# Two attention layers without staged operands: masks added ahead by GpSimd, values in the transposes' bank, pool mixing in halves, branches merged by tile pairs

## The chip, the cores and the metric

The kernel runs on 1 core of one Trainium2 chip. The metric is device time in microseconds for one execution. Engines: TensorE (PE, with its weight loads as PEld), VectorE (DVE), ScalarE (ACT), GpSimd (POOL) and SyncE (SP), which issues the stream of weights. Each engine executes its own queue in order, and engines wait for each other by semaphores.

## What is computed

The reference runs two layers of a first block (256 tokens, width 1024) and then one layer of a second block. The change lies in the first block, of which this is the core:

```python
for l in range(DEPTH):                       # 2 layers
    h = rms_norm(x, norm_g[l])
    proj = h @ w_in[l]
    (pool_u, pool_z, aq, ak, av, az, iq, ik, iw, mq, mz, gates) = jnp.split(proj, split_points, axis=-1)
    y_pool = multi_scale_pool(pool_u, pool_w[l], pool_scale[l]) * silu(pool_z)
    # 8 heads of 64; the indexer picks 64 of the admissible keys of each token
    y_attn = dsa_attention(aq, ak, av, iq, ik, iw, rel_bias) * silu(az)
    mk, mv = split(rms_norm(mem, mem_norm_g[l]) @ w_mem_kv[l])
    y_mem = memory_attention(mq, mk, mv) * silu(mz)          # 4 heads of 128
    g = sigmoid(gates)                                        # 3 x 1024 columns
    merged = g0 * (y_pool @ w_branch[l, 0]) + g1 * (y_attn @ w_branch[l, 1]) + g2 * (y_mem @ w_branch[l, 2])
    x = x + merged @ w_out[l]
```

The attention's logits are q k / 8 plus a bias by relative position, with keys that the indexer did not pick masked out. multi_scale_pool takes trailing means over 2, 4, 8 and 16 tokens and maps each group of 128 channels by its own matrix.

## The kernel before

**The weight stream.** All weights of 1024 rows come as blocks of 128 columns (512 KB) through four slots. A block goes through a fixed chain: SyncE loads raw[s]; ScalarE converts it to the rounded upper part w_hi (split_hi, L264); VectorE forms the rest w_lo (split_lo, L270); TensorE makes 24 matmuls of 256 tokens with it (block_cols): h_hi and h_lo by w_hi (L284, L285) and h_hi by w_lo (L299). Conversions run two blocks ahead (`ahead`): in step s of a group of four, ScalarE and VectorE convert the block of slot s + 2. ScalarE or VectorE takes the result out of PSUM (evac, L345). For tokens in rows, block_rows takes two slots at once (L330 to L335), and evac_rows takes its two results out one after the other, each behind the conversion of its own step.

**A layer** has 20 groups G to G + 19 of four blocks: index queries, q (qT), k (kT), v; the gates az, pz, mz; the pool's input pu; memory queries (mqT); then six groups for the 24 gate blocks, beside which the softmax of the six pairs runs: four pairs of attention heads (hp) and two pairs of memory heads (mp); then three groups of branch blocks, which need y_hi and y_lo; then two groups of w_out.

**A pair** runs so. GpSimd copies q and k of the pair into `stage` (st_q, st_k, L437 and L438), behind its own pooling (L418 to L432) for the first pair of a layer. TensorE forms the logits in PSUM banks 0 and 1 (free_ps[0], free_ps[1]; L1417, L1419) and adds the mask by a matmul with an identity (L1418, L1420), then three gate blocks, the transposes of the probabilities into banks 2 and 3 (L1428), the fourth gate block, and the values into bank 0 (L1434 to L1436). VectorE converts the lower part of slot 2, adds the bias to the logits (L999, L1001, four instructions), takes the row maxima; ScalarE makes the exponentials (L618), evicts the first gate block, converts slot 3; VectorE makes the lower part of slot 3 and normalises (L982). ScalarE copies the transposed probabilities to SBUF. After the values, VectorE multiplies them with the gate az (L1012) and splits the product into y_hi and y_lo; the next pair's logits wait for that product (pv_used). Between the fourth and fifth pair, TensorE mixes the pool (L1442) and VectorE takes that out (L1022).

**The branches.** For each of twelve blocks VectorE multiplies the result with the gate into `soft` (L1053) and GpSimd adds that to `merged` (L453), which it cleared before. All branch blocks wait for all six y's and for all gates. At the end ScalarE rounds `merged` in two halves into hS_hi (L654), VectorE forms hS_lo (L1060), and first_blocks starts w_out with two blocks, half by half (L318 is its lower part). Then VectorE adds each w_out result to x (L1067), and ScalarE squares it for the next norm.

Of the kernel before, what the change touches and what calls it, by code (L numbers as in the profile page):

```python
# [78 lines left out]
def build(nc, a, out):  # L79

    with ExitStack() as ctx:
# [8 lines left out]
        free_ps = [ctx.enter_context(nc.psum_tensor(f"free_ps{i}", [P, 512], F32)) for i in range(4)]  # L90
# [20 lines left out]
        with ExitStack() as one:  # L111
# [15 lines left out]
            with ExitStack() as win:  # L127
                y01_hi = sb("y01_hi", [P, 2, 4, S], F32R, win)
                sum_a = sb("sum_a", [P, POOLG, PAD + S], scope=win)
                sum_b = sb("sum_b", [P, POOLG, PAD + S], scope=win)  # L130
            y_hi = sb("y_hi", [P, 3, 4, S], F32R, one)
# [10 lines left out]
            st_q, st_k = stage[:, 0:S], stage[:, S:2 * S]  # L142
            st_v = stage[:, 2 * S:3 * S].rearrange("p (t n) -> p t n", t=2)
            st_mq = stage[:, 0:512].rearrange("p (h n) -> p h n", h=2)
            st_mv = stage[:, 512:1024].rearrange("p (t n) -> p t n", t=2)
# [10 lines left out]
        with ExitStack() as two:  # L156
# [66 lines left out]
        qk_staged, v_staged, logit_done, max_ready, exp_ready, prob_ready, softT_done, softT_ready, pv_done, pv_used = (  # L223
            sem(n) for n in ("qk_staged", "v_staged", "logit_done", "max_ready", "exp_ready", "prob_ready",
# [4 lines left out]
        part_used, mhi_ready, mlo_ready = (sem(n) for n in ("part_used", "mhi_ready", "mlo_ready"))  # L229
# [72 lines left out]
        def first_blocks(pe, G, free, free_at, r_hi, r_lo, parts):  # L302
# [3 lines left out]
            for half in range(2):  # L306
                for s in range(AHEAD):
                    if half == 0:
                        pe.wait_ge(hi_ready, 4 * G + s + 1)
                        pe.wait_ge(free, free_at + s)  # L310
                    if s == 0:
                        pe.wait_ge(parts[0], parts[1] + half)
                    for k in range(4 * half, 4 * half + 4):
# [85 lines left out]
        def _(pool):  # L399
# [6 lines left out]
            pool.sem_inc(part_used, 2)  # L406
# [3 lines left out]
            for l in range(0, LAYERS):  # L410
                E0 = SLOTS + 4 * MEM_GROUPS + ACT_EVACS * l

                pool.wait_ge(blk_done, SLOTS + 4 * (G0 + LAYER_GROUPS * l))
# [21 lines left out]
                for hp in range(0, 4):  # L435
                    pool.wait_ge(logit_done, 6 * l + hp + 1)
                    nc.gpsimd.tensor_copy(st_q, qT[:, bass.ds(hp, 1), :])  # L437
                    nc.gpsimd.tensor_copy(st_k, kT[:, bass.ds(hp, 1), :]).then_inc(qk_staged, 1)  # L438
                    pool.wait_ge(pv_done, 6 * l + hp + 1)
                    nc.gpsimd.tensor_copy(st_v, v[:, :, bass.ds(hp * P, P)]).then_inc(v_staged, 1)  # L440

                for mp in range(0, 2):
                    pool.wait_ge(pv_done, 6 * l + 4 + mp + 1)
                    nc.gpsimd.tensor_copy(st_mq, mqT[:, bass.ds(2 * mp, 2), :]).then_inc(qk_staged, 1)
                    nc.gpsimd.tensor_copy(st_mv, mv[:, bass.ds(l, 1), :, bass.ds(mp * 2 * P, 2 * P)]).then_inc(v_staged, 1)
                nc.gpsimd.drain()
                nc.gpsimd.memset(merged, 0.0)
                nc.gpsimd.drain()
                for br in range(0, 3):
                    for s in range(SLOTS):  # L450
                        pool.wait_ge(dve_evac, SLOTS + DVE_EVACS * l + 4 * br + s + 1)
# [1442 lines left out]
```

## Time and profile before

| | us |
|---|---|
| median of 3 runs | 1473.35 (1471.16 to 1473.35) |
| profiled execution | 1474.33 |
| its span, first to last instruction | 1472.5 |
| TensorE busy in the span | 1330.4 (90%) |
| VectorE busy | 857.8 (58%) |
| ScalarE busy | 633.0 (43%) |
| GpSimd busy | 263.2 (18%) |
| mean granted clock of TensorE, as a share of full speed | 0.947 |

Times within the trace are microseconds from the span's start. A matmul's duration includes the time to its last output, so matmuls overlap; the distance from start to start is what one costs in a row of them. Layer 0 lies from about 83 to 393 us, layer 1 from 393 to 697, then the second block. A releaser named behind an idle time is the event that came last before the instruction.

### The profile page before, as it was taken

The page shows a single profiled execution, that of the slowest core. Times are in us where ns is not written, and L with a number is a line of the kernel's source. Part 1 is how long each engine was busy: PE and PEld are TensorE (multiplying, and loading weights), DVE is VectorE, ACT ScalarE, POOL GpSimd, SP SyncE. Part 2 cuts the span into 40 slices and gives each one's busy share as a digit, 9 for nine tenths or more (in the row PEclk, how much of TensorE's full clock was granted, in tenths as well). Part 3 has the DMA queues.
Part 4 walks back from the last instruction along what each step waited for, and adds up shares of the span by engine and source line. Part 5 has one row for each costly group of instructions (what it writes and reads, how often), then busy time and mean ns, then how long its engine had stood idle before and what let it go on. Part 6 is the DMA issues. An engine that isn't in the chain of part 4 may idle for free.

```text
span 1472.5 us, 28707 instructions
## 1 busy us (share of the span) xinstructions
PE 1330.4 (90%) x12138; PEld 1267.3 (86%) x12138; DVE 857.8 (58%) x1352; ACT 633.0 (43%) x1040; POOL 263.2 (18%) x259
## 2 busy tenths in 40 slices
PE   4989989989899989998769889999999899799997
PEld 3979978989799978898559788999989899799997
DVE  4434745656536545564499776666656566555544
ACT  5424534443444444434526553333323453544533
POOL 0000040007000220152042244425235000000000
PEclk9989998999899989999889999999999899899999
DMA  4625553334445623344224332222222354355553
GB/s 171 210 83 170 176 168 101 115 130 158 138 143 162 193 92 129 122 164 144 83 86 137 107 116 84 76 88 67 94 76 70 116 172 157 127 189 186 187 190 126
DMA packets 59119, 195.13 MB, mean 133 GB/s; under 512 B 6248, under 2 KB 13928, under 8 KB 58736
## 3 DMA queue, kind: packets, MB, share of 16 engines
q1 hardware_dynamic: 49248, 179.33, 37.2%
q10 hardware_dynamic: 9440, 12.90, 2.6%
q8 instruction: 97, 1.59, 0.4%
q0 software_dynamic: 304, 1.07, 0.3%
q14 instruction: 30, 0.25, 0.1%
HBM read 189.06 MB, written 4.21 MB: 131 GB/s over the span
## 4 chain that ended last, share of the span: by engine, by line
PE 74%; DVE 13%; ACT 5%; issue 2%; DVEq 2%; POOL 2%; POOLq 1%; DMA 1%; ACTq 0%
PE stream_ps L284 15%; PE stream_ps L285 15%; PE stream_ps L299 11%; DVE w_lo L270 5%; PE stream_ps L278 4%; PE stream_ps L280 3%; PE stream_ps L279 3%; DVE qkvT L1114 2%; ACT w_hi L264 2%; PE free_ps L1657 2%; PE stream_ps L1488 2%; PE free_ps L1674 1%; PE stream_ps L1746 1%; DVEq L1120 1%; PE free_ps L370 1%
## 5 line engine op out<-in xcount | busy, mean ns | idle before, releaser
L270 DVE TENSOR_TENSOR w_lo<-raw,w_hi 128x1024 fp32r<-128x1024 f32 x342 | 430.7, 1266 | 319.7 <-ACT w_hi L264 316.2
L284 PE MATMUL stream_ps<-h_hi,w_hi 128*128 128x256 f32 (+1 forms) x1632 | 418.1, 292 | 21.2 <-DVE h_lo L1081 14.4
L285 PE MATMUL stream_ps<-h_lo,w_hi 128*128 128x256 f32 (+1 forms) x1632 | 412.9, 289 | 0.0
L264 ACT ACTIVATE w_hi<-raw 128x1024 fp32r<-128x1024 f32 x342 | 358.5, 1053 | 61.3 <-PE stream_ps L1488 44.8
L284 PEld LDWEIGHTS stream_ps<-h_hi,w_hi 128*128 128x128 f32 x1632 | 320.5, 196 | 24.7 <-issue 22.8
L285 PEld LDWEIGHTS stream_ps<-h_lo,w_hi 128*128 128x128 f32 x1632 | 320.5, 196 | 0.4 <-issue 0.2
L299 PE MATMUL stream_ps<-h_hi,w_lo 128*128 128x256 f32 (+1 forms) x1552 | 219.7, 284 | 21.3 <-DVE w_lo L270 21.3
L299 PEld LDWEIGHTS stream_ps<-h_hi,w_lo 128*128 128x128 f32 x1552 | 201.3, 191 | 22.3 <-DVE w_lo L270 22.2
L278 PE MATMUL stream_ps<-h_hi,w_hi 128*128 128x256 f32 (+1 forms) x384 | 122.5, 319 | 8.5 <-DVE cx L1165 8.5
L280 PE MATMUL stream_ps<-h_hi,w_lo 128*128 128x256 f32 (+1 forms) x384 | 111.5, 290 | 0.0
L279 PE MATMUL stream_ps<-h_lo,w_hi 128*128 128x256 f32 (+1 forms) x384 | 111.5, 290 | 0.0
L278 PEld LDWEIGHTS stream_ps<-h_hi,w_hi 128*128 128x128 f32 x384 | 75.0, 195 | 14.2 <-issue 10.8
L1238 DVE TENSOR_TENSOR xy<-xy,free_ps 64x128 f32<-64x128 f32 x180 | 44.7, 283 | 68.1 <-PE free_ps L1675 53.9
L279 PEld LDWEIGHTS stream_ps<-h_lo,w_hi 128*128 128x128 f32 x384 | 75.6, 197 | 0.1
L280 PEld LDWEIGHTS stream_ps<-h_hi,w_lo 128*128 128x128 f32 x384 | 75.5, 197 | 0.0
L809 ACT ACTIVATE n<-free_ps 64x128 f32<-64x128 f32 x80 | 22.0, 274 | 108.0 <-PE free_ps L1657 107.1
L1114 DVE SCALAR_TENSOR_TENSOR qkvT<-st_raw,gains,qkvT 128x272 f32<-128x272 f32 x96 | 65.5, 724 | 3.3 <-ACT qkvT L696 0.6
L511 POOL TENSOR_TENSOR lvl<-lvl,cst 128x256 f32<-128x256 f32 x60 | 53.7, 917 | 74.9 <-DVE lvl L1198 42.3
L453 POOL TENSOR_TENSOR wide<-wide,soft 128x512 f32<-128x512 f32 x24 | 52.9, 2205 | 56.4 <-DVE soft L1053 56.4
L284 PE MATMUL stream_ps<-y_hi,w_hi 128*128 128x256 f32 x192 | 49.4, 288 | 4.5 <-issue 4.5
L418 POOL TENSOR_TENSOR sum_a<-pu 128x1024 f32<-128x1024 f32 x2 | 3.8, 1891 | 257.1 <-ACT pu L345 257.1
L285 PE MATMUL stream_ps<-y_lo,w_hi 128*128 128x256 f32 x192 | 49.3, 289 | 0.0
(335 smaller groups left out, 2225.5 us busy)
## 6 DMA issues: line engine op xcount, KB each, us to landing
raw<-stream_dram SPq DMA_DIRECT2D x342, 512.0 KB, 3.3
gate_spill<-gate_out ACTq DMA_DIRECT2D x16, 128.0 KB, 1.9
xT<-xT_dram ACTq DMA_DIRECT2D x1, 1088.0 KB, 9.9
stage<-wik_dram ACTq DMA_DIRECT2D x2, 544.0 KB, 4.0
mem_raw<-memT_dram ACTq DMA_DIRECT2D x1, 1024.0 KB, 6.5
hankel<-rel_scratch POOLq DMA_DIRECT2D x1, 1024.0 KB, 10.6
x_spill<-xT ACTq DMA_DIRECT2D x1, 1024.0 KB, 4.8
gb<-gate_spill ACTq DMA_DIRECT2D x1, 1024.0 KB, 6.2
```

The source lines that it names most:

```text
L264: nc.scalar.activation(w_hi[s][:, :, :], raw[:, s, :].rearrange("p (k n) -> p k n", k=KT), ACT.Copy).then_inc(hi_ready, 1)
L270: nc.vector.tensor_tensor(w_lo[s][:, :, :], raw[:, s, :].rearrange("p (k n) -> p k n", k=KT), w_hi[s][:, :, :].bitcast(F32), ALU.subtract) ...
L278: nc.tensor.matmul(ps, l_hi, r_hi, start=first, stop=False)
L279: nc.tensor.matmul(ps, l_hi, r_lo, start=False, stop=False)
L280: return nc.tensor.matmul(ps, l_lo, r_hi, start=False, stop=last)
L284: nc.tensor.matmul(ps, l_hi, r_hi, start=first, stop=False)
L285: nc.tensor.matmul(ps, l_hi, r_lo, start=False, stop=False)
L299: mm = nc.tensor.matmul(ps, w_lo[s][:, k, :], r_hi[:, k, :], start=False, stop=k == KT - 1)
L453: nc.gpsimd.tensor_tensor(mg, mg, soft[:, s % 2, :].rearrange("p (k n) -> p k n", k=2), ALU.add).then_inc(part_used, 1)
L511: nc.gpsimd.tensor_tensor(lvl[:, lvl_slot(level), hs, :], lvl[:, 0, hs, :], col(5 + level).unsqueeze(1).broadcast_to([P, 4, C]), ALU.mult) ...
L1114: op = nc.vector.scalar_tensor_tensor(out=acc, in0=st_raw[:, m % SLOTS, tap:tap + T], scalar=gains[:, bass.ds(G_CONV + 40 * i + 5 * m + ta ...
L1238: op = nc.vector.tensor_tensor(part, part, src, ALU.subtract)
```

## The change

- **Staging.** `stage` holds only the index weights (wik). TensorE reads qT, kT, v, mqT and mv itself; GpSimd's copies are gone.
- **Masks.** GpSimd adds the mask to the bias of a pair's two heads into `masked` (two buffers): for pairs 0 and 1 as soon as the mask is there, ahead of the pooling; for pairs 2 and 3 behind it, once VectorE has used a buffer. TensorE's mask matmuls are gone. The four PSUM banks are one tensor (free_all), so VectorE adds scale and `masked` to both heads in one instruction, and ScalarE copies both banks of transposes in one.
- **Order of TensorE.** Logits of pair i + 1 come before the values of pair i; the values go to bank 2, whose transposes ScalarE has copied by then. The pool mixing comes in two halves, behind the second gate block of pairs 2 and 3, into banks 0 and 1, and has its own buffer `mixed`.
- **Row blocks.** ScalarE converts both next slots before it evicts the two results, for the memory's values and for v; the index's relu and sums move with that.
- **Branches.** Each branch waits only for its own y's and for the gates of its blocks. VectorE writes the first branch into `merged` directly; GpSimd adds the second; VectorE adds the third, and each pair of tiles is then rounded by ScalarE (in the last branch's loop) and its remainder formed by VectorE. first_blocks takes four quarters instead of two halves there, and makes the lower-part matmuls of the earlier quarters before the last one (in its other uses too, with two halves).

The core of the diff; first the banks and the helper for the first blocks of a group:

```diff
-        free_ps = [ctx.enter_context(nc.psum_tensor(f"free_ps{i}", [P, 512], F32)) for i in range(4)]
+        free_all = ctx.enter_context(nc.psum_tensor("free_ps", [P, 4, 512], F32))
+        free_ps = [free_all[:, i, :] for i in range(4)]
...
-        def first_blocks(pe, G, free, free_at, r_hi, r_lo, parts):
+        def first_blocks(pe, G, free, free_at, r_hi, r_lo, parts, count=2):
...
+            step = KT // count
+            for part in range(count):
                 for s in range(AHEAD):
...
+                    for k in range(step * part, step * part + step):
                         with_hi(stream_ps[s][:, 0:n], w_hi[s][:, k, :], r_hi[:, k, :], r_lo[:, k, :], k == 0)
+                if part == count - 2:
+                    for s in range(AHEAD):
+                        pe.wait_ge(lo_ready, 4 * G + s + 1 + SLOTS)
+                        for k in range(KT - step):
+                            nc.tensor.matmul(stream_ps[s][:, 0:n], w_lo[s][:, k, :], r_hi[:, k, :], start=False, stop=False)
             for s in range(AHEAD):
-                pe.wait_ge(lo_ready, 4 * G + s + 1 + SLOTS)
-                for k in range(KT):
+                for k in range(KT - step, KT):
```

GpSimd:

```diff
+                def mask_heads(hp):
+                    at = masked[:, hp % 2, :, :]
+                    heads = bias[:, 2 * hp:2 * hp + 2, :]
+                    both = lambda cols: mask[:, cols].unsqueeze(1).broadcast_to([P, 2, cols.stop - cols.start])
+                    nc.gpsimd.tensor_tensor(at[:, :, 0:P], heads[:, :, P:2 * P], both(slice(0, P)), ALU.add)
+                    nc.gpsimd.tensor_tensor(at[:, :, P:3 * P], heads, both(slice(P, 3 * P)), ALU.add).then_inc(masked_ready, 1)
+                pool.wait_ge(mask_ready, l + 1)
+                for hp in range(2):
+                    if l:
+                        pool.wait_ge(masked_used, 4 * l - 1 + hp)
+                    mask_heads(hp)
...
-                for hp in range(0, 4):
-                    pool.wait_ge(logit_done, 6 * l + hp + 1)
-                    nc.gpsimd.tensor_copy(st_q, qT[:, bass.ds(hp, 1), :])
-                    nc.gpsimd.tensor_copy(st_k, kT[:, bass.ds(hp, 1), :]).then_inc(qk_staged, 1)
...
-                nc.gpsimd.memset(merged, 0.0)
...
+                for hp in range(2, 4):
+                    pool.wait_ge(masked_used, 4 * l + hp - 1)
+                    mask_heads(hp)
+                for s in range(SLOTS):
+                    pool.wait_ge(dve_evac, SLOTS + DVE_EVACS * l + 4 + s + 1)
+                    mg = merged[:, 2 * s:2 * s + 2, :]
+                    nc.gpsimd.tensor_tensor(mg, mg, soft[:, s % 2, :].rearrange("p (k n) -> p k n", k=2),
+                                            ALU.add).then_inc(part_used, 1)
```

ScalarE:

```diff
-                for s in range(SLOTS):
+                for s in range(0, SLOTS, 2):
                     ahead(split_hi, act, 2 * l + 1, s)
-                    evac_rows(act, 2 * l + 1, s, mv[:, l, :, s * P:(s + 1) * P])
+                    ahead(split_hi, act, 2 * l + 1, s + 1)
+                    for j in (s, s + 1):
+                        evac_rows(act, 2 * l + 1, j, mv[:, l, :, j * P:(j + 1) * P])
...
                 for br in range(0, 3):
                     for s in range(SLOTS):
                         ahead(split_hi, act, G + 15 + br, s)
-                act.wait_ge(blk_done, SLOTS + 4 * (G + 15))
-                for half in range(2):
-                    act.wait_ge(part_used, 12 * l + 12 - 2 + 2 * half + 2)
-                    ks = slice(4 * half, 4 * half + 4)
-                    nc.scalar.activation(hS_hi[:, ks, :], merged[:, ks, :], ACT.Copy, scale=0.5).then_inc(mhi_ready, 1)
+                        if br == 2:
+                            act.wait_ge(merged_ready, 4 * l + s + 1)
+                            ks = slice(2 * s, 2 * s + 2)
+                            nc.scalar.activation(hS_hi[:, ks, :], merged[:, ks, :], ACT.Copy, scale=0.5).then_inc(mhi_ready, 1)
```

VectorE:

```diff
-                            dve.wait_ge(logit_done, 6 * l + hp + 2)
...
+                            dve.wait_ge(logit_done, 6 * l + hp + 1)
+                            dve.wait_ge(masked_ready, 4 * l + hp + 1)
+                            nc.vector.scalar_tensor_tensor(out=soft[:, :, 0:384], in0=free_all[:, 0:2, 0:384], scalar=ATTN_SCALE,
+                                                           in1=masked[:, hp % 2, :, :], op0=ALU.mult, op1=ALU.add).then_inc(masked_used, 1)
...
+                    dve.wait_ge(pv_done, 6 * l + hp + 1)
+                    if hp == 0:
+                        dve.wait_ge(pooled_ready, l + 1)
+                    nc.vector.tensor_tensor(soft[:, 0, 0:S], free_ps[2][:, 0:S], az[:, hp, :], ALU.mult).then_inc(pv_used, 1)
...
+                def merged_lo(s):
+                    dve.wait_ge(mhi_ready, 4 * l + s + 1)
+                    ks = slice(2 * s, 2 * s + 2)
+                    nc.vector.scalar_tensor_tensor(out=hS_lo[:, ks, :], in0=merged[:, ks, :], scalar=0.5,
+                                                   in1=hS_hi[:, ks, :].bitcast(F32), op0=ALU.mult, op1=ALU.subtract).then_inc(mlo_ready, 1)
                 for br in range(0, 3):
                     for s in range(SLOTS):
                         ahead(split_lo, dve, G + 15 + br, s)
...
+                        if br == 1 and s >= 2:
+                            dve.wait_ge(part_used, 4 * l + s - 1)
+                        if br == 2:
+                            dve.wait_ge(part_used, 4 * l + 4)
+                        nc.vector.scalar_tensor_tensor(out=merged[:, ks, :] if br == 0 else part,
...
+                        if br == 2:
+                            nc.vector.drain()
+                            nc.vector.tensor_tensor(merged[:, ks, :], merged[:, ks, :], part, ALU.add).then_inc(merged_ready, 1)
+                            if s:
+                                merged_lo(s - 1)
+                merged_lo(SLOTS - 1)
```

TensorE:

```diff
+                logits(0)
+                for i in range(6):
                     for s in range(SLOTS):
+                        block_cols(pe, G + 9 + i, s, act_evac, E + 36 + 4 * i + s + 1, hS_hi, hS_lo)
+                        if s == 1 and i in (2, 3):
+                            pool_mix(i - 2)
                         if s == 2:
+                            transposes(i)
+                    if i < 5:
+                        logits(i + 1)
+                    values(i)
                 for br in range(0, 3):
+                    pe.wait_ge(y_ready, 8 * l + (5, 6, 8)[br])
...
+                first_blocks(pe, G + 18, dve_evac, D_wo + 1, hS_hi, hS_lo, (mlo_ready, 4 * l + 1), 4)
```

In the new functions of TensorE, logits(i) waits for the maxima of pair i - 1 (for the last memory pair, its predecessor's exponentials), and for pairs 3 and 4 also for VectorE's reading of a pool half; transposes(i) waits for the probabilities of pair i and the gate product of pair i - 1; values(i) waits for ScalarE's copy of the transposes; pool_mix(i) waits for the pooling and for the maxima of pair i + 2.

## Rows read from the trace of the kernel before

**Rows 1.** Who waited for whom, TensorE, second layer: us in total, times, longest:

```profile
PE free_ps L1417 <- DVE soft L1012: 1.8, 3, 0.6
...
PE stream_ps L284 <- issue: 2.2, 1, 2.2
PE free_ps L1461 <- DVE soft L982: 2.1, 1, 2.1
...
PE stream_ps L330 <- ACT w_hi L264: 1.4, 1, 1.4
...
PE free_ps L1451 <- DVE soft L1041: 0.9, 1, 0.9
```

**Rows 2.** Instructions of TensorE in time: start, us, line, form, idle before, releaser:

```profile
216.49 0.76 PE L1417 MATMUL free_ps<-stage 64*128 64x128 f32 x2 [5.51 <-POOL stage L438]
```

**Rows 3.** Chain of waits in time, one pair boundary, pool mixing: start, us, what:

```profile
254.93 0.46 PE free_ps L1417 x2
255.39 0.16 PE free_ps L1418
...
256.18 0.21 PE free_ps L1420
...
257.81 0.12 PE stream_ps L284
...
266.29 0.66 PE free_ps L1428 x6
...
287.42 1.94 PE free_ps L1442 x8
```

**Rows 4.** Stretches of layer 0: length, busy time and instructions by engine, clock, DMA:

```profile
211.00:236.30 25.30, 19.78 (x126) 17.24 (x126) 8.35 (x16) 10.40 (x21) 6.11 (x12) 0.80 0.26 86
236.30:254.36 18.06, 17.44 (x126) 15.62 (x126) 9.44 (x19) 7.96 (x19) 1.15 (x3) 0.91 0.37 117
254.36:270.90 16.54, 15.94 (x126) 14.43 (x126) 9.39 (x19) 7.94 (x19) 1.14 (x3) 1.00 0.40 128
...
324.30:362.30 38.00, 35.83 (x288) 35.66 (x288) 23.07 (x26) 12.15 (x12) 24.14 (x11) 0.96 0.49 165
362.30:371.30 9.00, 6.51 (x42) 6.25 (x43) 4.20 (x5) 2.00 (x2) 2.36 (x2) 0.81 0.35 107
```

**Rows 5.** VectorE and GpSimd in time: mask and start of the pooling:

```profile
180.21 0.36 DVE L971 TENSOR_SCALAR mask<-softT 128x384 bf16<-128x384 f32 x1
...
200.20 1.89 POOL L418 TENSOR_TENSOR sum_a<-pu 128x1024 f32<-128x1024 f32 x1 [117.68 <-ACT pu L345]
...
201.02 2.15 DVE L270 TENSOR_TENSOR w_lo<-raw,w_hi 128x1024 fp32r<-128x1024 f32 x1 [1.61 <-ACT w_hi L264]
```

**Rows 6.** VectorE in time, gate product of pair 0 and softmax of pair 1:

```profile
236.31 0.42 DVE L1012 TENSOR_TENSOR soft<-free_ps,az 128x256 f32<-128x256 f32 x1 [0.85 <-PE free_ps L1436]
...
237.72 1.22 DVE L270 TENSOR_TENSOR w_lo<-raw,w_hi 128x1024 fp32r<-128x1024 f32 x1
240.33 0.29 DVE L999 SCALAR_TENSOR_TENSOR soft<-free_ps,bias 128x128 f32<-128x128 f32 x1 [1.39 <-PE free_ps L1420]
...
247.35 1.01 DVE L982 TENSOR_SCALAR soft<-soft,stat 128x128 f32<-128x128 f32 x4
```

**Rows 7.** ScalarE in time, the same pair:

```profile
242.85 0.40 ACT L618 ACTIVATE soft<-soft,stat 128x128 f32<-128x128 f32 x1 [6.28 <-DVE stat L1007]
...
244.62 0.36 ACT L345 ACTIVATE gates<-stream_ps 128x256 f32<-128x256 f32 x1
```

**Rows 8.** VectorE in time, last branch product and first residual add:

```profile
362.33 0.69 DVE L1053 SCALAR_TENSOR_TENSOR soft<-gates,stream_ps 128x512 f32<-128x512 f32 x1 [1.01 <-PE stream_ps L1488]
...
371.29 0.42 DVE L1067 TENSOR_TENSOR xT<-stream_ps,xT 128x256 f32<-128x256 f32 x1 [2.50 <-PE stream_ps L318]
```

**Rows 9.** The page's costliest groups: busy, mean ns, idle before:

```profile
L264 ACT ACTIVATE w_hi<-raw 128x1024 fp32r<-128x1024 f32 x342 | 358.5, 1053 | 61.3 <-PE stream_ps L1488 44.8
```

**Rows 10.** VectorE in time, end of the prologue:

```profile
78.72 1.23 DVE L270 TENSOR_TENSOR w_lo<-raw,w_hi 128x1024 fp32r<-128x1024 f32 x1 [4.84 <-ACT w_hi L264]
```

More of the change, by code:

```diff
@@ L141, in build @@
             wik = stage[:, :].rearrange("p (k n) -> p k n", k=KT)
[L142 to L145, printed above, removed]
+            masked = sb("masked", [P, 2, 2, 384], scope=one)
             pool_w = sb("pool_w", [P, POOLG, P], scope=one)
@@ L1025, in _ @@
-                op = split_y(soft[:, :, :].rearrange("p i (j n) -> p (i j) n", j=2), y_hi[:, 0, :, :], y_lo[:, 0, :, :])
-                op.then_inc(mixed_used, 1)
-                nc.vector.drain()
+                        if s == 2 and hp >= 2:
+                            i = hp - 2
+                            dve.wait_ge(mixed_done, 2 * l + i + 1)
+                            for j in range(2):
+                                g = 2 * i + j
+                                op = nc.vector.scalar_tensor_tensor(out=mixed[:, j, :], in0=free_ps[i][:, j * S:(j + 1) * S],
+                                                                    scalar=gains[:, G_POOL + POOLG * l + g:G_POOL + POOLG * l + g + 1],
+                                                                    in1=pz[:, g, :], op0=ALU.mult, op1=ALU.mult)
+                            op.then_inc(mixed_used, 1)
+                            split_y(mixed[:, :, :], y_hi[:, 0, 2 * i:2 * i + 2, :], y_lo[:, 0, 2 * i:2 * i + 2, :]).then_inc(y_ready, 1)
@@ new lines, in transposes, with values @@
+                def transposes(i):
+                    pe.wait_ge(prob_ready, 6 * l + i + 1)
+                    if i:
+                        pe.wait_ge(pv_used, 6 * l + i)
+                    for j in range(2):
+                        for c in range(3 if i < 4 else 4):
+                            mm = nc.tensor.transpose(free_ps[2 + j][:, c * P:(c + 1) * P], soft[:, j, c * P:(c + 1) * P], ident)
+                    mm.then_inc(softT_done, 1)
+                def values(i):
+                    pe.wait_ge(softT_ready, 6 * l + i + 1)
+                    for j in range(2):
+                        if i < 4:
+                            o, vc = free_ps[2][HD * j:HD * j + HD, :], slice(i * P + HD * j, i * P + HD * j + HD)
+                            nc.tensor.matmul(o[:, 0:P], v[:, 0, vc], softT[:, j, 0:P], start=True, stop=True)
+                            nc.tensor.matmul(o[:, P:S], v[:, 0, vc], softT[:, j, P:2 * P], start=True, stop=False)
+                            mm = nc.tensor.matmul(o[:, P:S], v[:, 1, vc], softT[:, j, 2 * P:3 * P], start=False, stop=True)
+                        else:
+                            h = 2 * (i - 4) + j
+                            for t in range(2):
+                                o = free_ps[2][:, j * S + t * P:j * S + (t + 1) * P]
+                                for m in range(2):
+                                    mm = nc.tensor.matmul(o, mv[:, l, m, h * P:(h + 1) * P], softT[:, j, (2 * t + m) * P:(2 * t + m + 1) * P],
+                                                          start=m == 0, stop=m == 1)
+                    mm.then_inc(pv_done, 1)
@@ new lines, in pool_mix @@
+                def pool_mix(i):
+                    if i == 0:
+                        pe.wait_ge(pooled_ready, l + 1)
+                        pe.wait_ge(poolw_in, 16 * (l + 1))
+                    pe.wait_ge(max_ready, 6 * l + i + 3)
+                    for j in range(2):
+                        g = 2 * i + j
+                        mm = nc.tensor.matmul(free_ps[i][:, j * S:(j + 1) * S], pool_w[:, g, :], pu[:, g, PAD:], start=True, stop=True)
+                    mm.then_inc(mixed_done, 1)
```

240 lines of the change are left out of this document (82 added, 158 removed).

## The prediction

> **What bounds the kernel now.** I read first who waited for whom on TensorE in the second layer [rows 1], then TensorE's rows around its longest wait [rows 2], then one boundary between two head pairs in the chain of waits [rows 3], and the layer cut into stretches with their clock [rows 4]. The reader is to see that TensorE bounds the layers, at 2.83 us a weight block (three blocks lie between 257.81 and 266.29), that each wait sits at a place this change touches, and that a wait costs more than itself: after several of them the granted clock is below 1, which is the 1.2 GHz level in part of the stretch. The second layer repeats the first, so I count one layer and double. The sum is made against the profiled execution, 1474.3 us; the median of the three runs is 1.0 below it.
>
> **What goes, per layer.**
> - GpSimd's staging. Logits wait until GpSimd has finished the pooling and copied q and k: 5.5 us [rows 2]. Read from qT and kT directly they wait for nothing, since TensorE's own blocks already required those tiles.
> - At each pair boundary TensorE finishes the values, waits for their product with the gate and only then starts the next logits, at 254.93, because both use bank 0 [rows 3]: three times 0.6, and 0.9 at the memory pair [rows 1]. With the values in bank 2 and the next logits ahead of them, all 2.7 go.
> - The 2.1 before the first memory pair's transposes, and the 2.2 listed as "issue" before the branches, which is the wait for the last y [rows 1]. The branch blocks now ask for y in three steps, and the last is only needed eight blocks later. Together 4.3.
> - The mask's matmuls: 0.16 and 0.21 per head [rows 3], 0.74 a pair, four pairs: 3.0. GpSimd adds them to the bias instead, off the path: for pairs 0 and 1 ahead of the pooling, for 2 and 3 behind it; the mask is written at 180.21 and GpSimd pools from 200.20 on [rows 5], so two pairs of 768 columns have 20 us. Behind VectorE's new wait for them stand the softmax and the lower parts, so lateness would reach TensorE whole.
> - The pool mixing's eight matmuls, 1.9 [rows 3], move in halves into waits of TensorE (below). If the waits are absent, 1.9 stays.
> - The clock's share. The stretch of pair 0 lasts 25.3 us [rows 4], less the wait 19.8, where its work at full clock is 15.9 (logits 2.9, four blocks 11.3, and 1.7 for transposes and values, which is what pair 2's 16.54 leave with its wait): 3.9. Pair 1 takes 18.06 at clock 0.91 against 16.54 for pair 2 at 1.00: 1.5. The branch stretch takes 38.0; 2.2 are waited and 12 blocks are 34.0: 1.8. Together 7.2, if the clock then stays up.
> - The row blocks of v: the second conversion is queued on ScalarE behind the eviction of the first pair; 1.4 [rows 1].
>
> Sum: 5.5 + 2.7 + 4.3 + 3.0 + 1.9 + 7.2 + 1.4 = 26.0 us.
>
> **What comes, per layer.** First, a wait in every pair but the first. VectorE's queue is in order: the gate product and split of pair i, then the lower part of slot 2, then the softmax of pair i+1. Before, that ran beside the logits and the wait ahead of them. Now the logits come before the values, so nothing of TensorE is left to cover it. From the end of the values: product and split 1.41 (236.31 to 237.72), lower part 1.23, scores to exponentials 2.52 (240.33 until ScalarE starts at 242.85) [rows 6, 7], exponentials 1.77 until the gate's eviction at 244.62 [rows 7], then conversion and lower part of slot 3 and the normalising, 3.74 (until 247.35 + 1.01) [rows 6]: 10.7. One fused score instruction for four and pipelining between neighbours may take 0.4 off. TensorE has three blocks before it needs the probabilities, 8.5: a wait of 1.8 to 2.2. Five pairs, the memory pairs taken alike: 9 to 11, I take 9.5. The pool halves lie inside two of these waits.
>
> Second, the turn from the branches to w_out. From the last branch product at 362.33 to the first residual add at 371.29 are 8.96 us [rows 8]. The new order removes GpSimd's add and the halves there, but makes a ring: in the last branch ScalarE queues the conversion of the next-but-one block behind the rounding of the tile pair just merged, and VectorE queues the merging behind that block's lower part. One round: rounding of 512 columns 0.55 (half of the 1.05 of a 1024-column conversion [rows 9]), conversion 1.05, lower part 1.23, product 0.7, sum 0.65, four hand-overs 0.1 together: 4.3 against 2.83 for the block. The first sum stands about 1.8 after block 0, so the fourth at 1.8 + 3 x 4.3 = 14.7 and the third remainder, which follows it on VectorE, at 15.2. TensorE's ends: third quarters 0.95, their lower parts 1.4, last quarters 0.95 and 0.24 (0.118 a matmul), so 18.7, which is 10.2 after the last block (8.5). That is 1.3 worse, up to 2.9 if TensorE's idle time ahead of slot 1, which is converted only in the last round, lowers the clock as idle time does at this place now (0.81) [rows 4]; I take 2.0. I found no term here that gains.
>
> Third, the clock. Idle stretches of 2 us among blocks lowered it at the turn [rows 4], not before the memory pair's transposes. I take one new drop, 1.5; bounds 0 and 8 (five at 1.6).
>
> Fourth, GpSimd is still pooling during pair 0's softmax. A lower part took 2.15 instead of 1.23 while GpSimd pooled [rows 5, 6]; pair 0 has only some 0.2 of slack. Bounds 0 and 1.4, I take 0.4. The Trainium skill (SBUF — State Buffer, "Who interferes with whom") says that a VectorE instruction with two SBUF inputs and a GpSimd one that reads SBUF exclude each other for a whole instruction. The row of 2.15 agrees with it, since the lower part has two such inputs. By that rule the new score instruction, with one input in PSUM, would not be held; only the two lower parts would, and the term would be the 1.4 at most.
>
> Sum: 9.5 + 2.0 + 1.5 + 0.4 = 13.4. Net per layer 12.6, twice 25.2.
>
> **Outside the layers.** The two memory row pairs have the same wait of 1.4 each. At the end of the prologue VectorE's last lower part, waited for until 78.72 [rows 10], no longer stands ahead of the bias copies: 0 to 1.5, I take 1.3. Together 4.1. first_blocks' new order moves lower-part matmuls ahead in the second block too; no wait for the second half stands there now: 0. ScalarE's loads of wik and pool_w keep their place in its queue and wait for less: 0.
>
> **The Trainium skill against the change.** GPSIMD Engine Reference (4.1 Engine selection) puts two-input elementwise work on VectorE, as GpSimd is about twice as slow for it. No row here shows the mask sum on either engine. The rule would speak against moving it only if GpSimd's sums were late; at the cover named above they are not, so the sum stays the same.
>
> **Forecast.** 1474.3 - 25.2 - 4.1 = 1445.0; at the median 1444.0 us.
>
> **Rivals.**
> - The softmax chain stays covered. For it: TensorE never waited for probabilities in pairs 0 to 3 before. Against it: the chain above is 2 us longer than three blocks. Without the five waits (9.5 a layer): 1444.0 - 19.0 = 1425.
> - The clock falls after every new wait: 6.5 more a layer, 1457. For it, the drops at the turn [rows 4]; against it, the undisturbed memory pair.
> - The change doesn't free TensorE from GpSimd: if the masked bias is late, VectorE waits where TensorE did, 5.5 and the 3.9 of clock come back in each layer: 1463. Against it: those 20 us.
> - Slower than before: the six pairs, now a mix of waits and short matmuls, hold TensorE at 1.2 GHz. A block then takes 2.83 longer. The net gain is 14.6 a layer with the prologue's half, so it decides from five uncovered blocks of the twenty in pairs 1 to 5; at ten, less 9.5 hidden in the waits, it costs 2 x 18.8: 1482. Against it: pairs 2 and 3 run at clock 1.00 with similar matmuls.
>
> **How the numbers follow.** Chances: forecast 0.52, covered chain 0.20, clock after every wait 0.16, GpSimd late 0.05, slower 0.05, none of the gains 0.02. The range reaches from the covered chain, 1425, to the clock's case with the turn at its upper bound, 1459; it leaves about 0.12 outside at the top and a little below. About 0.2% is what a measurement of this kernel can tell from no change: faster 0.93, same 0.02, slower 0.05.
>
> **What would show it.** In the changed kernel's trace: no wait of TensorE for GpSimd before the first logits and clock 1.00 through pair 0; five waits of about 2 us before the transposes, released by VectorE's normalising; logits followed by values without a gap; twelve branch blocks starting at once; a ring of 4.3 us at the last branch and 10 us or more to the first residual add. The prediction is wrong if the transposes don't wait, if the rounds of the last branch take 2.8, or if the clock sits at half through whole pairs.

## The result, and the profile after

The changed kernel takes 1461.07 us (median of 4 runs, 1459.23 to 1463.63); the one before 1473.35. The ratio is 0.992, 95% interval 0.9902 to 0.9939: faster by 12.3 us, where 29 were forecast. The profiled execution took 1461.5, its span is 1459.7. The page of the changed kernel, its span and the row of the granted clock in 40 slices:

```profile
span 1459.7 us, 28564 instructions
PEclk9999999999799999997889897999999899899999
```

The second half of the program is the second block. In it, five equal steps of a recurrence (the delta rule, on chunks of the tokens) run one after the other, each with a few weight blocks and a part of a short convolution beside it: VectorE adds up three shifted and scaled copies of a row (the taps) and multiplies the sum with the result of a weight block, into the tile `cx`. TensorE needs the PSUM buffer that this product reads for a later block. I cut both traces at the same first matmuls on TensorE (second norm, first logits, first branch block, norm behind w_out, first block of the second half, first key product of the delta rule's first step, first branch block behind the five steps). Lengths in us:

| stretch | before | after | gained | forecast |
|---|---|---|---|---|
| start to layer 0's second norm | 90.77 | 86.07 | 4.7 | 4.1 |
| that norm to the first logits, layers 0 and 1 | 125.73, 122.13 | 115.95, 119.03 | 9.8, 3.1 | 6.9 each |
| six pairs | 109.97, 109.72 | 105.43, 105.47 | 4.5, 4.2 | 5.9 each |
| branches and w_out | 62.61, 62.34 | 61.97, 61.94 | 0.6, 0.4 | -0.2 each |
| norm behind it | 9.87, 22.61 | 10.55, 24.54 | -0.7, -1.9 | 0 |
| second half up to the delta rule | 157.71 | 157.72 | 0.0 | 0 |
| the delta rule's five steps | 302.05 | 313.78 | **-11.7** | 0 |
| the rest | 297.02 | 297.27 | -0.2 | 0 |

Each row is one profiled execution. Up to the delta rule, though, a_late09, a_late19 and a_taps below are the changed kernel, and from the second norm on they repeat its rows within 0.1 us; b_taps and b_late19 repeat those of the kernel before within 0.3.

At the second half's first block the changed kernel leads by 24.8 us (690.96 against 715.75), near the 29.3 forecast. It gives 11.7 of them back in 300 us of code that the change doesn't touch. The layers first.

Who TensorE waited for in the second layer (us in total, times, longest), changed kernel; it answers [rows 1]:

```profile
PE free_ps L1461 <- DVE soft L995: 9.7, 6, 2.3
PE free_ps L1398 <- DVE gates L381: 5.1, 1, 5.1
PE stream_ps L283 <- ACT w_hi L263: 3.0, 1, 3.0
PE stream_ps L283 <- DVE h_lo L1062: 0.3, 1, 0.3
```

GpSimd, the pair boundaries, the last y and the row blocks are gone. In their place, in each layer, stand six waits for the probabilities (L1461), and 3.0 at the turn. The queue behind one of the six, pair 1 of layer 0 (start, us, engine, line, form), first VectorE, then ScalarE's first exponential, then TensorE's transposes; they answer [rows 6, 7]:

```profile
221.19 0.42 DVE L1034 TENSOR_TENSOR soft<-free_ps,az 128x256 f32<-128x256 f32 x1 [3.28 <-PE free_ps L1472]
...
222.60 1.23 DVE L269 TENSOR_TENSOR w_lo<-raw,w_hi 128x1024 fp32r<-128x1024 f32 x1
223.74 0.95 DVE L1011 SCALAR_TENSOR_TENSOR soft<-free_ps,masked 128x768 f32<-128x768 f32 x1
```

```profile
226.63 0.40 ACT L631 ACTIVATE soft<-soft,stat 128x128 f32<-128x128 f32 x1 [6.04 <-DVE stat L1017]
```

```profile
232.20 1.31 PE L1461 MATMUL free_ps<-cst,soft 128*128 128x128 f32 x6 [2.33 <-DVE soft L995]
```

VectorE idles 3.28 us for the values, and only then come gate product, lower part and scores, though the logits had been there since 220.1. At the turn VectorE's second sums (L1082) of the last three tile pairs and the first residual add, which answer [rows 8]:

```profile
338.65 0.69 DVE L1082 TENSOR_TENSOR wide<-wide,soft 128x512 f32<-128x512 f32 x1
...
342.90 0.69 DVE L1082 TENSOR_TENSOR wide<-wide,soft 128x512 f32<-128x512 f32 x1
...
347.15 0.69 DVE L1082 TENSOR_TENSOR wide<-wide,soft 128x512 f32<-128x512 f32 x1
...
352.34 0.43 DVE L1091 TENSOR_TENSOR xT<-stream_ps,xT 128x256 f32<-128x256 f32 x1 [1.62 <-PE stream_ps L322]
```

One round is 4.25 us, and the first add stands 10.7 behind w_out's first matmul (341.62), which follows the last branch block at once: the ring as forecast.

TensorE's logits of one pair in layer 0, with the first weight block behind them: first before (all between are logits and mask matmuls; it answers [rows 3]), then after (`wide` holds qT):

```profile
254.93 0.46 PE L1417 MATMUL free_ps<-stage 64*128 64x128 f32 x2 [0.61 <-DVE soft L1012]
...
257.56 0.36 PE L284 MATMUL stream_ps<-h_hi,w_hi 128*128 128x256 f32 x1
```

```profile
202.02 0.50 PE L1445 MATMUL free_ps<-kT,wide 64*128 64x128 f32 x4
202.35 0.61 PE L1446 MATMUL free_ps<-kT,wide 64*128 64x256 f32 x4
202.89 0.39 PE L283 MATMUL stream_ps<-h_hi,w_hi 128*128 128x256 f32 x1
```

At full clock they took 2.63 us and now take 0.86: the change gains 1.8 a pair here, where 0.74 was forecast for the mask's matmuls.

In pair 0, GpSimd works beside VectorE. VectorE's rows of pair 0, and the scaling of the row maxima in pairs 0 and 1 with GpSimd's second mask sum beside it:

```profile
203.49 1.81 DVE L269 TENSOR_TENSOR w_lo<-raw,w_hi 128x1024 fp32r<-128x1024 f32 x1 [1.39 <-ACT w_hi L263]
205.23 0.94 DVE L1011 SCALAR_TENSOR_TENSOR soft<-free_ps,masked 128x768 f32<-128x768 f32 x1
...
207.36 1.03 DVE L1017 TENSOR_SCALAR stat<-stat 128x4 f32<-128x4 f32 x1
...
225.87 0.73 DVE L1017 TENSOR_SCALAR stat<-stat 128x4 f32<-128x4 f32 x1
```

```profile
207.20 1.17 POOL L422 TENSOR_TENSOR masked<-bias,mask 128x512 f32<-128x512 f32 x1
...
225.40 1.17 POOL L422 TENSOR_TENSOR masked<-bias,mask 128x512 f32<-128x512 f32 x1
```

Then what was not forecast. Stretches of the changed kernel (length, busy time and instructions of PE, PEld, DVE, ACT and POOL, granted clock, DMA): both layers' way from norm to logits, the first layer's pairs, the five steps, and 20 us inside the first step:

```profile
86.00:202.00 116.00, 115.93 (x944) 114.00 (x944) 67.89 (x107) 54.20 (x84) 14.67 (x17) 0.97 0.45 159
379.90:499.00 119.10, 119.02 (x944) 116.59 (x944) 67.85 (x107) 54.13 (x84) 14.69 (x17) 0.95 0.44 155
202.00:307.40 105.40, 95.62 (x752) 91.06 (x752) 58.74 (x100) 49.58 (x106) 7.95 (x10) 0.95 0.35 125
848.60:1162.40 313.80, 304.27 (x4186) 282.99 (x4184) 192.29 (x396) 100.60 (x200) 109.36 (x128) 0.92 0.22 78
874.30:894.50 20.20, 20.20 (x215) 18.75 (x214) 8.04 (x18) 5.06 (x12) 5.42 (x9) 0.50 0.17 60
```

The same of the kernel before:

```profile
90.70:216.40 125.70, 118.80 (x944) 116.28 (x944) 67.42 (x108) 56.69 (x87) 15.35 (x21) 0.95 0.48 156
398.90:521.00 122.10, 115.20 (x944) 112.85 (x944) 67.39 (x108) 56.65 (x87) 15.38 (x21) 0.98 0.50 160
216.40:326.40 110.00, 102.91 (x768) 94.43 (x768) 59.07 (x112) 49.08 (x109) 7.93 (x15) 0.94 0.34 111
873.40:1175.50 302.10, 292.42 (x4184) 272.01 (x4185) 193.05 (x396) 100.53 (x200) 111.36 (x128) 0.96 0.25 81
898.00:918.00 20.00, 20.00 (x350) 18.35 (x350) 12.57 (x32) 6.94 (x16) 7.50 (x10) 1.00 0.29 94
```

The steps have the same instructions and the same waits, but the clock is 0.92 instead of 0.96. In the first step of the changed kernel it is 0.50, the 1.2 GHz level, for 20 us, in which TensorE gets through 215 matmuls; the kernel before makes 350 in 20 us from the same wait on. The place is the same in both: a wait of 0.97 us for the short convolution's product (cx). TensorE around it, first before, then after:

```profile
897.86 0.36 PE L278 MATMUL stream_ps<-h_hi,w_hi 128*128 128x256 f32 x1 [0.98 <-DVE cx L1165]
...
898.99 0.30 PE L1674 MATMUL free_ps<-n,xy 64*64 64x32 f32 x4
...
899.80 0.39 PE L278 MATMUL stream_ps<-h_hi,w_hi 128*128 128x256 f32 x1
```

```profile
873.08 0.36 PE L277 MATMUL stream_ps<-h_hi,w_hi 128*128 128x256 f32 x1 [0.97 <-DVE cx L1189]
...
874.21 0.43 PE L1706 MATMUL free_ps<-n,xy 64*64 64x32 f32 x4
...
875.63 0.58 PE L277 MATMUL stream_ps<-h_hi,w_hi 128*128 128x256 f32 x1
```

Same matmuls, same wait, in one trace at full clock, in the other at half. Each of the five steps has this wait (4.9 us in both traces). In the changed kernel the clock falls after all five, in the one before after the last three. From one step's first key product to the next it takes 58.6 us where the clock stays up and 61.6 where it falls; the changed kernel's first step, with the long fall, takes 67.5.

### The profile page after: what moved, and what is told of

Same layout as the page of the kernel before. It is cut to its first block, busy times and chain, and to the rows that moved or that the text cites. A ratio compares the mean times of both kernels' runs of the same rounds, so it can differ in the third digit from the quotient of the medians.

```text
span 1459.7 us, 28564 instructions
## 1 busy us (share of the span) xinstructions
PE 1326.2 (91%) x12106; PEld 1270.9 (87%) x12106; DVE 866.8 (59%) x1344; ACT 631.1 (43%) x1032; POOL 224.9 (15%) x225
## 4 chain that ended last, share of the span: by engine, by line
PE 69%; DVE 15%; ACT 7%; DVEq 4%; issue 3%; DMA 1%; POOL 0%; ACTq 0%; POOLq 0%
PE stream_ps L283 13%; PE stream_ps L284 13%; PE stream_ps L298 10%; DVE w_lo L269 6%; PE stream_ps L277 4%; PE stream_ps L279 3%; ACT w_hi L263 3%; PE stream_ps L278 3%; DVE qkvT L1138 2%; PE free_ps L1689 2%; PE free_ps L1706 2%; PE stream_ps L1778 1%; PE free_ps L374 1%; DVEq L1144 1%; PE free_ps L1707 1%
## 5 line engine op out<-in xcount | busy, mean ns | idle before, releaser
L298 PE MATMUL stream_ps<-h_hi,w_lo 128*128 128x256 f32 (+1 forms) x1552 | 221.3, 286 | 21.3 <-DVE w_lo L269 21.3
L298 PEld LDWEIGHTS stream_ps<-h_hi,w_lo 128*128 128x128 f32 x1552 | 202.7, 192 | 22.3 <-DVE w_lo L269 22.2
L279 PE MATMUL stream_ps<-h_hi,w_lo 128*128 128x256 f32 (+1 forms) x384 | 114.5, 298 | 0.0
L279 PEld LDWEIGHTS stream_ps<-h_hi,w_lo 128*128 128x128 f32 x384 | 78.5, 205 | 0.0
L458 POOL TENSOR_TENSOR wide<-wide,soft 128x512 f32<-128x512 f32 x8 | 17.6, 2206 | 196.3 <-DVE soft L1076 196.3
L421 POOL TENSOR_TENSOR masked<-bias,mask 128x256 f32<-128x256 f32 x8 | 7.4, 919 | 260.9 <-DVE mask L984 228.1
## 6 DMA issues: line engine op xcount, KB each, us to landing
hankel<-rel_scratch POOLq DMA_DIRECT2D x1, 1024.0 KB, 10.6
```

Of the source, the lines that this page charges most:

```text
L279: return nc.tensor.matmul(ps, l_lo, r_hi, start=False, stop=last)
L298: mm = nc.tensor.matmul(ps, w_lo[s][:, k, :], r_hi[:, k, :], start=False, stop=k == KT - 1)
```

## The experiments

**Theory:** the wait in the step makes the clock fall or not by where it comes in time; the change only moved it, by 25 us. **Rivals:** something that was altered slows the second half wherever it stands; or the steps' short matmuls lower the clock, wait or not.

**a_late09 and a_late19.** Only the first step's key products are repeated, with the same result (`half == 0` dropped for a_late19):

```
-                    for j, wide_j, _ in heads:
+                    for j, wide_j, _ in heads * (1 + (1 if t == 0 and half == 0 else 0)):
```

> The changed kernel, with one half of the first step's key products of the delta rule made twice (the same values again, 0.93 us more of full TensorE work); nothing else differs. The five steps of the delta rule last 313.8 us in the changed kernel and 302.1 in the one before (from the first key product to the first branch block), with the same 0.97 us wait for the convolution's product in each step; in the changed kernel the clock falls after all five of these waits, in the one before after three. Theory (where the wait falls in time decides whether the clock drops; the changed kernel only arrives 25 us earlier, and so elsewhere): moved by 0.93 us the steps lose another sum of clock, 301 to 308 us, and the kernel takes 1450 to 1457 us although it does more. Rival (something that the change altered makes the second block slower wherever it starts): 314.7 us and 1462.0.

Measured: 1447.87 us (1445.44 to 1449.96); ratio to before 0.9818, 0.9794 to 0.9843. 0.93 us **more** work makes the kernel 13.2 us faster, even a little more than the theory allowed. The clock falls after the last two waits only. Its steps (columns as above):

```profile
848.80:1148.70 299.90, 290.35 (x4201) 270.10 (x4200) 192.89 (x396) 100.58 (x200) 112.38 (x128) 0.98 0.25 81
```

> The same with both halves of the first step's key products made twice: 1.87 us more work ahead of the steps. Theory: the steps lose another sum of clock than 20 us, between 300 and 309 us in all, the kernel 1451 to 1459. Rival: 315.7 us and 1463.0.

Measured: 1452.8 us (1451.83 to 1454.34), 0.9853, 0.9831 to 0.9876. The clock falls after the last four waits. Its steps, with the five waits of 0.97 still there:

```profile
848.30:1155.00 306.70, 297.22 (x4218) 276.46 (x4216) 193.00 (x396) 100.54 (x200) 110.36 (x128) 0.95 0.24 79
```

**b_late19.** The repeated products could also help by being work, not by their delay. So the same edit, both halves, in the kernel before.

> The kernel before, with both halves of the first step's key products of the delta rule made twice: 1.87 us more of full TensorE work ahead of the five steps, the wait of 0.97 us in each step left as it is. In it the clock falls after three of the five waits; they stand where they spare the first two. Theory (the place in time decides): moved by 1.87 us more of the five waits, the first among them, lower the clock; steps of 306 to 316 us instead of 302.1, the kernel 1478 to 1487. Rival (the clock doesn't depend on where the steps begin): steps of 303.9 us, the kernel 1475.3.

Measured: 1485.85 us (1480.63 to 1489.32), 1.0075, 1.0049 to 1.0102: 1.87 us of work cost 12.5. The clock falls after the first four waits, for 20 us after the third. Its steps:

```profile
874.50:1187.20 312.70, 303.06 (x4216) 282.14 (x4216) 192.93 (x396) 100.58 (x200) 109.38 (x128) 0.93 0.24 78
```

The altered code is not the cause: the same 1.87 us take 7 us off the steps of one kernel and add 10.6 to those of the other.

**a_taps and b_taps.** The wait itself goes. VectorE's three taps move from ahead of the product to the place behind the first right side, where it idles 2.72 us:

```
                 if s == 2:
-                    nc.vector.drain()
-                    nc.vector.tensor_scalar(acc, x(0), gains[:, bass.ds(G_SC + 3 * j, 1)], None, ALU.mult)
...
+                    if not early:
+                        taps(j)
                     nc.vector.drain()
...
                 fill(1)
                 right_side(0)
+                taps(PRE + t)
```

> The changed kernel, with VectorE making the three taps of the short convolution one place earlier in each step (where it idles 2.7 us) and only the product with the block's output in the old place: what TensorE waits 0.97 us for in each step comes some 2.5 us sooner. Theory (the clock falls because of that wait): no wait and no half clock in the five steps, 293.8 - 4.9 = 289 us, the kernel 1461.1 - 4.9 - 20 = 1436. Rival (the short matmuls of the steps lower the clock, wait or not): only the waits go, 1456.

Measured: 1435.83 us (1434.34 to 1436.59), 0.9734, 0.9708 to 0.976. The steps:

```profile
848.10:1136.20 288.10, 283.43 (x4185) 263.77 (x4184) 191.20 (x396) 100.62 (x200) 111.56 (x128) 0.99 0.26 84
```

> The kernel before, with the same move of the taps. Theory: steps of 289 us, the kernel 1473.4 - 4.9 - 8.3 = 1460, and 24 to 25 us above the changed kernel with its taps moved, which is the lead of 24.8 us that the changed kernel has at the first block of the second half. Rival (the short matmuls lower the clock): 1468.5; rival (the change itself slows the second block): still 12 above the changed kernel with its taps moved.

Measured: 1461.67 us (1461.09 to 1472.17), 0.9931, 0.9906 to 0.9957. Five of the eight runs lie between 1461.1 and 1461.7, three between 1469.2 and 1472.2; the profile is of 1461.09. The steps:

```profile
873.80:1161.90 288.10, 283.39 (x4184) 263.80 (x4184) 191.37 (x396) 100.59 (x200) 111.55 (x128) 1.00 0.26 85
```

The short matmuls of these steps don't lower the clock by themselves. Without the wait a step takes 57.6 us, which is the 58.6 of an undisturbed one less the wait, and the five take 288.1 wherever they begin: in the profiles of the six kernels that have this move they begin between 807.7 and 874 and last 288.05 to 288.14. The two kernels now lie 25.8 apart, as much as the change gained ahead of the steps (24.8), and 1.0 more. With waits of 4.9 the clock cost the steps 9.1 us before (302.1 - 4.9 - 288.1) and 20.8 after.

**b_direct.** One part of the change alone, on b_taps: TensorE reads q, k, v and the memory's tiles in place.

```
-                        nc.tensor.matmul(free_ps[j][:, 0:P], st_q[rows, 0:P], st_k[rows, 0:P], start=True, stop=False)
+                        nc.tensor.matmul(free_ps[j][:, 0:P], qT[rows, hp, 0:P], kT[rows, hp, 0:P], start=True, stop=False)
...
-                    pool.wait_ge(logit_done, 6 * l + hp + 1)
-                    nc.gpsimd.tensor_copy(st_q, qT[:, bass.ds(hp, 1), :])
...
```

> The kernel before with its taps moved (1461.7 us), and of the change only one part: logits and values read q, k, v and the memory's tiles where they are, GpSimd copies nothing; the order of values and logits, the banks, the masks on TensorE and the turn stay as before. Theory (the wait for GpSimd goes whole, and where nothing else waits the clock gives some back): the stretch from the second norm to the first logits 5.5 us shorter in each layer, no wait of TensorE before the first logits, and the pairs up to 3.4 us shorter a layer by the clock; the kernel 1444 to 1451. Rival (VectorE waits where TensorE did, as GpSimd is still pooling): a new wait of 2 us or more before the first transposes, under 4 us a layer in all, 1454 to 1458.

Measured: 1451.01 us (1450.18 to 1451.72), 0.9845, 0.9822 to 0.9867: 10.7 below b_taps, at the theory's upper end. From norm to logits, both layers:

```profile
91.70:212.00 120.30, 118.81 (x944) 116.40 (x944) 66.17 (x107) 54.10 (x84) 10.01 (x12) 0.95 0.45 153
...
394.80:515.40 120.60, 119.14 (x944) 116.55 (x944) 66.22 (x107) 54.08 (x84) 10.03 (x12) 0.95 0.44 153
```

Layer 0 gains 5.5 (125.8 in b_taps) at an unchanged 0.95. Layer 1 gains 1.5 only (122.1 in b_taps, at 0.98), as the clock is now 0.95 there too. The pairs gain another 1.5 and 2.6. No new wait stands ahead of the transposes of pair 0. The term of 5.5 holds; the clock moved beside it. With the mask's matmuls kept, a pair's logits take 2.63 as before.

**a_scores.** Is it VectorE's order that makes the six waits? On a_taps, the scores of pair i+1 go ahead of the product of pair i, and those of pair 0 ahead of its first lower part; the product goes to another tile:

```
+                    scores(hp + 1)
                     dve.wait_ge(pv_done, 6 * l + hp + 1)
...
-                    nc.vector.tensor_tensor(soft[:, 0, 0:S], free_ps[2][:, 0:S], az[:, hp, :], ALU.mult).then_inc(pv_used, 1)
+                    nc.vector.tensor_tensor(mixed[:, 0, :], free_ps[2][:, 0:S], az[:, hp, :], ALU.mult).then_inc(pv_used, 1)
```

> The changed kernel with its taps moved (1435.8 us), and on VectorE the scores of pair i+1 (scale, mask, maxima) placed ahead of the product and split of pair i's values instead of behind them and a lower part; the product goes to another tile. Theory (the waits before the transposes, 9.8 us a layer in the changed kernel, come from this order in VectorE's queue): the exponentials start 3 us earlier, the six waits a layer all but go, 1435.8 - 2 x 9.8 = 1416, a little less where the clock then stays up, and the first block of the second half comes some 20 us earlier. Rival (ScalarE's order, conversions and evictions around the exponentials, sets the waits): half of them stay, 1426.

Measured: 1402.87 us (1402.46 to 1405.42), 0.952, 0.9504 to 0.9536. The pairs of layer 0:

```profile
201.30:291.20 89.90, 89.90 (x753) 86.49 (x752) 58.86 (x100) 50.87 (x106) 8.01 (x10) 1.00 0.44 143
```

All six waits are gone, and with them 15.6 us a layer: 9.8 of waits, and 5.8 in which TensorE was busy at a lower clock with the same matmuls. The theory holds, but I had allowed the clock too little: 33 us came instead of 19.6.

**a_turn.** On a_taps, in the third branch the lower part goes behind product, sum and remainder:

```
-                        ahead(split_lo, dve, G + 15 + br, s)
+                        if br < 2:
+                            ahead(split_lo, dve, G + 15 + br, s)
...
-                            if s:
+                            if s == 3:
+                                merged_lo(2)
+                            ahead(split_lo, dve, G + 15 + br, s)
+                            if s in (1, 2):
                                 merged_lo(s - 1)
```

> The changed kernel with its taps moved, and in the third branch VectorE makes product, sum and the halves' remainders ahead of the lower part of the next-but-one block instead of behind it, which takes that block's conversion out of the ring of 4.25 us a tile pair. Theory (the ring sets the turn to w_out): rounds of 2.8 to 3.3 us, the first residual add 7 us after the last branch block instead of 10.1, some 3 us less a layer: 1430. Rival (VectorE's own work at this place is the bound): not over 1 us a layer, 1434 to 1436.

Measured: 1422.65 us (1420.48 to 1425.8), 0.9652, 0.9632 to 0.9672. Branches and w_out of layer 0, and layer 1 from norm to logits:

```profile
307.50:365.50 58.00, 57.35 (x483) 56.95 (x483) 38.21 (x48) 22.82 (x28) 7.92 (x4) 1.00 0.50 163
376.10:492.10 116.00, 115.93 (x944) 114.01 (x944) 67.83 (x107) 54.10 (x84) 14.64 (x17) 0.97 0.47 159
```

The ring was the bound: the rounds fall to 3.1, the first add comes 6.8 us behind w_out's first matmul, and the stretch is 4.0 shorter (62.0 in a_taps, at 0.97): 2.7 of waits and 1.3 of clock. Of the 13.2 us gained 8 are that; most of the rest is layer 1's way to the logits, 3.0 shorter by its clock, with no instruction of it changed.

**a_both.** All three moves.

> All three moves together on the changed kernel: taps, scores first, turn. Theory: the gains add, 1435.8 - 19.6 - 6 = 1410, up to 8 less where TensorE's clock keeps up without its waits. Rival (the clock takes back what the waits give, at other places): over 1418.

Measured: 1393.16 us (1390.54 to 1395.99), 0.9446, 0.9421 to 0.947: below both kernels and below either move alone, 17 under the sum that was expected. The gains that a_scores and a_turn measured, 33.0 and 13.2, would give 1389.7. Two of the four runs took 1390.5 and 1390.8, two 1395.6 and 1396.0. In the profile, which is of 1395.6, layer 1 from norm to logits is back at 0.95:

```profile
359.60:478.20 118.60, 118.52 (x945) 116.28 (x945) 67.90 (x107) 54.12 (x84) 14.70 (x17) 0.95 0.46 155
```

The same stretch lasts 116.0 in a_turn and 118.5 here, fully busy in both.

## Why the prediction was wrong

The direction and most steps were right; the time, 1444, was 17 too low and the range ended 2 below the result.

- **The failed step: the second half at nothing.** The prediction carried the layers' gain whole to the end and looked in the second half only for waits that the change makes ("first_blocks' new order ... 0"). That 0 holds for its part: up to the delta rule both kernels take 157.7. What failed is the assumption that code which isn't touched keeps its time when it begins 25 us earlier. That code held a wait of 0.97 us per step that cost 9.1 us of clock before and 20.8 after: 11.7 of the 17 that were missing. a_late09 has the changed kernel's every wait and stands at 1447.9, 4 above the forecast. Another 4.5 lie ahead of it, where 24.8 came of 29.3; that this is so near is in part luck, as misses both ways stand behind it (the next points).
- **The clock in the layers.** I took 7.2 a layer back and 1.5 as new drops. The pairs went from 0.94 to 0.95 only: from 215.4, 232.5 and 300.8 on, TensorE ran at 1.2 GHz, behind the three longest of the six new waits (2.3, 2.3 and 2.1 us); behind the three of 0.9 to 1.2 it did not. Length alone doesn't decide, as 0.97 was enough in the steps, and 2.1 before the memory pair's transposes in the kernel before was not. New drops cost 5.8 a layer (a_scores), inside my bounds of 0 and 8, but four times the 1.5 that I took. Of the rivals, the fall after every wait (1457) is right for half the waits. Late masks (1463) came nearest in time, but no wait for them stands in the trace.
- **Ahead of the logits.** The 5.5 (b_direct) and the 1.4 (no such wait is left) came, but with the clock the stretch gained 9.8 in layer 0 and 3.1 in layer 1, TensorE being busy throughout in both. The norms lost 0.7 and 1.9. I had the clock of both at 0.
- **The logits were a gain that I sized too small.** I counted the mask's matmuls alone, 3.0 a layer. A pair's logits fell by 1.77, so four pairs gained 7.1; b_direct, which keeps the mask's matmuls, keeps the 2.63. Without them the two heads' own matmuls stand next to each other, and all eight take 0.86 us where they took 2.1 with the mask's between them. Why they do is not tested. This 4.1 a layer hid the clock's miss: the pairs gained 4.5 and 4.2 for 5.9, though pair 0 waited 1.9 too long, and by what remains of the sum the clock gave nothing here, where I had 3.9 net (5.4 back, 1.5 lost).
- **The new waits.** The five behind a pair boundary were forecast at 9.5, with the pool halves inside two of them. They measure 7.5 of idle time, and the two halves take 0.9 each: 9.3, for the reason given, as a_scores removes them by VectorE's order alone. Pairs 2 and 3 wait 0.9, as their pool halves fill the rest. What was wrong is pair 0: it waits 2.3 where I took 0.4, with a bound of 1.4.
- **GpSimd beside VectorE.** By the rows above this makes some 1.4 of pair 0's wait. Its scores stand behind a lower part (203.49). That lower part, with two SBUF inputs, took 1.81 instead of 1.23; the score instruction, with one in PSUM, took 0.94 while GpSimd pooled and 0.95 in pair 1 without it. The Trainium skill's rule (SBUF — State Buffer, "Who interferes with whom") is borne out by both rows. The prediction expected only lower parts to be held. But the scaling of the maxima, four columns, took 1.03 and 0.73 where pairs 2 and 3 and the kernel before need 0.17, and both times it ended with GpSimd's mask sum. So the masks, which the prediction moved off the path, most likely cost 0.9 and 0.6 us on VectorE's way to the probabilities.
- **The turn.** 4.25 a round for 4.3, the first add 10.7 behind the branches for 10.2. The branches and w_out gained 0.6 and 0.4 a layer, not -0.2.
- **GpSimd's masks** were never late: no wait for them stands in the trace. The **prologue** gained 4.7 for 4.1.

The Trainium skill (TensorE: Matmul & The Clock Gate, Part 1) says that the gate's own timing is free-running and that the moment of a transition varies with where the work falls in it. That the place matters, a_late09, a_late19 and b_late19 show: 0.93 or 1.87 us of shift changed the steps by 7 to 14 us. That the timing doesn't follow the kernel's own start, they don't show: in the profiles of all seven kernels with the change the clock first falls in layer 0 between 0.3 and 0.6 us ahead of the second norm's first matmul. Nor does an edit have to move the work: the runs of b_taps, one kernel, lie up to 11 us apart, and which part of the program differs there isn't known. What the gate weighs in such a stretch these runs don't show.

## What to carry to other kernels

A gain reaches the end only if what lies behind it keeps its time: before predicting, list every short wait of TensorE behind the change, in code that isn't touched too, and price each with and without a fall of the clock. Take such waits out first (three taps moved to an idle place took 25 us off the changed kernel); then changes add up far better (a_scores and a_turn gave 33.0 and 13.2 alone, 42.7 together), and variants can be compared. Judge a change at the first common matmul behind it, not by the total alone.

## What was not expected of the hardware

A wait of 0.97 us among short matmuls was followed by 1.2 GHz for up to 20 us, or by nothing, as the start of the same code moved by 1 or 2 us. TensorE at 100% busy took 116.0 us or 118.5 for the same 944 or 945 recorded matmuls (granted clock 0.97 and 0.95). And more work was faster: 0.93 us added took 13.2 off. Eight matmuls of 64 rows, four for each head, took 0.86 us next to each other and 2.1 with matmuls of 128 rows between them.
